# Seven block products in all six feed-forward halves of a two-block network, weight sums on GpSimd, hosted running sums in PSUM

## What is computed

```python
def sq_relu_mlp(h, w1, w2):
    return jnp.square(jax.nn.relu(h @ w1)) @ w2            # network 1, both layers: 1024 -> 4096 -> 1024

def swiglu(x, w1, w3, w2):
    return (jax.nn.silu(x @ w1) * (x @ w3)) @ w2           # network 2, layer 0: 1024 -> 2816 -> 1024

hl = layer_norm(DEEPNORM_ALPHA * hl + m_l[5] * sq_relu_mlp(modulate(hl, m_l[3], m_l[4]), ffn_w1[i], ffn_w2[i]), ...)
m_l = jnp.split((s_lat @ ada_w[i] + ada_b[i])[:, None, :], 6, axis=-1)   # six quarters of 1024 columns
m_c = jnp.split(s_ctx @ ada_w[i] + ada_b[i], 6, axis=-1)
```

## Time and profile before

| | us |
|---|---|
| median of 3 runs | 3179.68 |
| lowest, highest run | 3177.56, 3181.84 |
| profiled execution, its own time | 3183.86 |
| its span in the trace | 3182.0 |
| PE busy | 3054.5 |
| DVE busy | 1339.1 |
| ACT busy | 544.2 |
| POOL busy | 109.1 |

### The profile page before, as it was taken

The page is one execution under the profiler, slowest core; times in us unless marked ns, Lnnn a source line. Parts: engine busy times, 40 slices in busy tenths (PEclk is TensorE's granted clock), DMA queues, the critical chain, the costliest instruction groups (busy, mean ns, idle before and its releaser), DMA issues.

```text
span 3182.0 us, 33283 instructions
## 1 busy us (share of the span) xinstructions
PE 3054.5 (96%) x13304; PEld 2064.1 (65%) x13304; DVE 1339.1 (42%) x3117; ACT 544.2 (17%) x1149; POOL 109.1 (3%) x84
## 2 busy tenths in 40 slices
PE   7999989999999999899999999999999989999999
PEld 2448444444466666788844655887446666999998
DVE  3576365467647777311122327775013442000011
ACT  0115110000033434121021321000012331000000
POOL 0000000000000000000000002342000000000000
PEclk9999999999999999899999999999999988999999
DMA  7550145566331222245431104454222012887785
GB/s 260 172 172 27 53 161 183 158 186 185 116 83 50 74 80 85 101 146 152 146 93 53 53 27 161 155 171 115 73 93 80 27 53 84 275 305 267 263 293 194
DMA packets 395321, 431.58 MB, mean 136 GB/s; under 512 B 15449, under 2 KB 307960, under 8 KB 395034
## 3 DMA queue, kind: packets, MB, share of 16 engines
q1 hardware_dynamic: 294320, 329.77, 31.9%
q10 hardware_dynamic: 100842, 99.62, 9.7%
HBM read 428.32 MB, written 1.05 MB: 135 GB/s over the span
## 4 chain that ended last, share of the span: by engine, by line
PE 90%; DVE 5%; ACT 2%; issue 1%; DMA 0%; DVEq 0%; ACTq 0%
PE bank L837 45%; PE bank L2578 10%; PE bank L2159 7%; PE bank L855 5%; PE bank L2592 4%; PE bank L863 4%; PE bank L528 2%; PE bank L1951 1%; DVE arena L573 1%; PE bank L1944 1%; PE bank L2560 1%; PE bank L2604 1%; PE bank L1548 1%; PE bank L1568 1%; PE bank L1936 1%
## 5 line engine op out<-in xcount | busy, mean ns | idle before, releaser
L837 PE MATMUL bank<-uT,slot 128*128 128x512 f32 (+2 forms) x2208 | 782.8, 511 | 0.0
L837 PE MATMUL bank<-arena,slot 128*128 128x512 f32 (+1 forms) x2016 | 692.9, 505 | 12.9 <-DVEq L2758 10.6
L837 PEld LDWEIGHTS bank<-uT,slot 128*128 128x128 f32 (+1 forms) x2208 | 414.8, 190 | 319.6 <-issue 296.5
L837 PEld LDWEIGHTS bank<-arena,slot 128*128 128x128 f32 x2016 | 386.2, 193 | 298.7 <-issue 274.5
L573 DVE SCALAR_TENSOR_TENSOR arena<-arena,sT 128x256 f32<-128x256 f32 x784 | 365.4, 521 | 7.4
L2578 PE MATMUL bank<-arena,slot 128*128 128x128 f32 x2816 | 317.8, 276 | 3.3 <-issue 2.9
L2578 PEld LDWEIGHTS bank<-arena,slot 128*128 128x128 f32 x2816 | 316.8, 193 | 5.9 <-issue 5.9
L2663 DVE TENSOR_TENSOR arena<-bank,halves 128x256 f32<-128x256 f32 (+1 forms) x48 | 19.3, 403 | 433.8 <-ACT halves L2624 433.8
L916 DVE SCALAR_TENSOR_TENSOR hT<-bank,mod,hT 128x256 f32<-128x256 f32 (+1 forms) x88 | 36.8, 456 | 370.3 <-PE bank L837 370.3
L855 PE MATMUL bank<-uT,slot 128*128 128x512 f32 (+1 forms) x448 | 165.2, 530 | 5.2 <-DVE uT L600 5.2
L2592 PE MATMUL bank<-slot,arena 128*128 128x256 f32 x704 | 153.3, 379 | 1.0 <-DVEq L145 1.0
(11 more groups left out here) (362 smaller groups left out, 2770.0 us busy)
## 6 DMA issues: line engine op xcount, KB each, us to landing
arena<-in_ada_w ACTq DMA_DIRECT2D x88, 1024.0 KB, 5.3
slot<-in_ffn_w SPq DMA_DIRECT2D x42, 2048.0 KB, 8.9
slot<-in_moe_w SPq DMA_DIRECT2D x32, 2048.0 KB, 10.0
slot<-in_moe_w SPq DMA_DIRECT2D x32, 1408.0 KB, 8.6
slot<-in_moe_w SPq DMA_DIRECT2D x16, 1536.0 KB, 9.0
slot<-in_ssd_w_in SPq DMA_DIRECT2D x32, 512.0 KB, 6.7
slot<-in_gla_w_in SPq DMA_DIRECT2D x6, 2048.0 KB, 10.3
slot<-in_ev_w_in SPq DMA_DIRECT2D x6, 2048.0 KB, 7.8
```

The lines of the kernel that those rows point to most:

```text
L837: ins = pe.matmul(bank[0:m, 0:t1 - t0], w[:, k, c0:c0 + m], x[:, k, t0:t1], start=(k == 0), stop=(k == kt - 1))
```

## The change

All six halves now run on one class `Seven` with a new order of products. A unit is a weight block of 2 MB (four tiles of 128 features in the hidden halves; 16 blocks of k and 256 features in the down halves of network 1), cut in 2 x 2 quarters; tokens are cut in two halves of 256 or 128 columns. POOL writes all four weight sums over the quarters of the slot; DVE makes four token sums per stage (twice per down half, which works its k in two chunks); ACT copies the first product to its place, and DVE adds the others there. ACT does relu and square on whole units. `Down` takes the place of `Residual` in the three down halves: it is `joined`, adds chunk by chunk to `hT` from `halves`, and has its own places for the norm. Hosted pieces are spread anew over all six halves (16, 16, 6, 6, 24 and 4), their places are counted in products, their sums run in the PSUM bank `ada_rows_bank` and are made four (seven) products ahead in two (four) parts. Some constants (1408 of 2368 columns) are loaded only at the start of `OddProject`.

```diff
-            ORDER = ("11", "12", "S2", "S1", "S3", "S4", "22")
+            ORDER = ("11", "12", "S1", "22", "S2", "S4", "S3")
+            TOKENS = {"S1": 1, "22": 2, "S3": 1}
+            def order(units):
+                first = [(q, name) for q in (0, 1) for name in ("11", "12")]
+                return first + [(q, name) for q in range(units) for name in Seven.ORDER if (q, name) not in first]
+            def token_sum(self, dve, step):
+                made = S("token_sums")
+                if step > 1:
+                    dve.wait_ge(made.sem, made.made)
+                out, a, b = {1: (self.t1, self.x12, self.x11), 2: (self.t2, self.x22, self.t1),
+                             4: (self.t4, self.t2, self.x21), 3: (self.t3, self.t2, self.x11)}[step]
+                dve.tensor_tensor(out, a, b, ALU.subtract).then_inc(*made.given())
+            def product(self, pe, bank, w, name, fresh, streamed=None):
+                if name in ("S1", "S2", "S4", "S3"):
+                    pe.wait_ge(*S("weight_sums").taken("pe"))
+                if fresh and name in self.TOKENS:
+                    pe.wait_ge(*S("token_sums").taken("pe", self.TOKENS[name]))
...
+                for u in us:
+                    for k in range(self.h):
+                        if streamed and u == 0:
+                            streamed()
+                        ins = pe.matmul(bank[:, u * n:u * n + n], a[:, k, u * P:u * P + P], x[:, k, :], start=(k == 0),
+                                        stop=(k == self.h - 1))
+            def pool(pool, B, w, at):
+                pool.tensor_tensor(a21, a21, a22, ALU.add).then_inc(*made.given())
+                B.full(pool, at("11"))
+                pool.wait_ge(made.sem, made.made)
+                pool.tensor_tensor(a11, a21, a11, ALU.subtract).then_inc(*made.given())
+                B.full(pool, at("12"))
+                pool.wait_ge(made.sem, made.made)
+                pool.tensor_tensor(a12, a12, a11, ALU.subtract).then_inc(*made.given())
+                B.full(pool, at("22"))
+                pool.tensor_tensor(a22, a22, a11, ALU.subtract).then_inc(*made.given())
+            def dve(dve, B, c, at, name):
...
+                elif name == "S2":
+                    ins = dve.tensor_tensor(c.second, c.second, c.both(bank), ALU.add)
+                elif name == "S4":
+                    ins = dve.tensor_tensor(c.c12, c.c22, c.part(bank), ALU.add)
+                else:
+                    ins = dve.tensor_tensor(c.second, c.second, c.both(bank), ALU.add)
...
+        class Down(Stage):
+            joined = True
+            pooled = True
...
+            def dve(self, dve, B, ch):
+                dve.wait_ge(*self.src.made(self.chunks[0][1]))
+                self.sevens[0].token_sum(dve, 1)
+                B.full(dve, -1)
+                for step in (2, 4, 3):
+                    self.sevens[0].token_sum(dve, step)
+                if self.src.guest:
+                    self.src.guest.dve(dve, ch)
+                self.norm.dve_begin(dve, ch)
+                self.norm.dve_ctx_sums(dve, ch)
+                for i, (c, u, name) in enumerate(self.order):
+                    Seven.dve(dve, B, Tiles(self.out), self.at(c, u), name)
+                    if c and u and name == "12":
+                        self.norm.dve_tile(dve, B, ch, 2 * u - 2)
+                        self.norm.dve_tile(dve, B, ch, 2 * u - 1)
...
+                    if name in ("S4", "S3"):
+                        B.freed(dve, i)
+                        j = int(name == "S3")
+                        ins = self.add(dve, j, 2 * u + j, 0, slice(0, LAT))
+                        if self.T == TOK:
+                            ins = self.add(dve, j, 2 * u + j, 1, slice(LAT, TOK))
...
+                    part_sum = guest_bank if self.in_bank else acc
...
-        stages += [hid, Residual(I["ffn_w2"][0], hid.hid, 32, M[0], 5, TOK, False,
-                                 AdaGuest(1, 0, all_six, spread, all_six), Norm(8, M[1], 0, TOK, True))]
+        hid = HiddenRelu2(I["ffn_w1"][0], TOK, AdaGuest(ada01[0:4], spread(8, 52, 16), hidden_guest, 4, 2))
+        stages += [hid, Down(I["ffn_w2"][0], hid, M[0], 5, Norm(8, M[1], 0, TOK, True),
+                             AdaGuest(ada01[4:6] + ada10[0:2], spread(5, 50, 16), down_guest, 4, 2))]
```

More of the change, by code:

```diff
@@ L511, in sides @@
             def sides(self, n):
[L513 removed]
+                return range(self.items[n][3])
             def summed(self, n):
@@ L549, in begin, with loads, sums @@
                     self.load(act, n)
[L551 to L559 removed]
+            def loads(self, act, place):
+                n = self.at.get(place + 1)
+                if n is not None and n + 2 < self.total:
+                    self.load(act, n + 2)
+            def sums(self, dve, ch, place):
+                for n, part in self.sum_at.get(place, ()):
                     g = self.first + n
                     if 0 in part:
[L562 removed]
+                        dve.wait_ge(guest_landed[g % 2], 16 * (g // 2 + 1))
                         if n >= 2:
@@ L976, in act @@
                        .then_inc(S("bias_loads").sem, 16)
-                for i in range(32):
-                    bank = B.full(act, i)
-                    if i >= 2:
-                        act.wait_ge(*S("free_a").taken("act"))
-                    act.activation(rl[i % 2][:, 0:self.T], bank[:, 0:self.T], ACT.Relu).then_inc(*B.free(i))
-                    if self.guest:
-                        self.guest.loads(act, (i,))
-                for i in range(2):
-                    act.wait_ge(*S("free_a").taken("act"))
+                for i, (q, name) in enumerate(self.order):
+                    if name == "11":
+                        Seven.act(act, B, Tiles(self.tiles(q)), i)
+                    if self.guest:
+                        self.guest.loads(act, i)
+                    if name == "S3":
+                        B.freed(act, i)
+                        h = self.tiles(q)
+                        ch.wait(ch(act.activation(h, h, ACT.Relu)))
+                        act.activation(h, h, ACT.Square).then_inc(*S("hid_done").given())
@@ L994, in dve @@
                 if self.guest:
                     self.guest.dve(dve, ch)
-                for k in range(KD if self.ctx else 0):
-                    bank = B.full(dve, 32 + k)
-                    dve.tensor_copy(hT[:, k, LAT:TOK], bank[:, 0:CTX]).then_inc(*B.free(32 + k))
         HQ = 4
```

629 lines of the change are left out of this document (342 added, 287 removed).

## The result

The changed kernel takes **3091.8 us** (median of four runs, 3090.0 to 3099.9) beside 3180.8 of the kernel before on the same chip: a ratio of 0.9726, 95% interval 0.9707 to 0.9745, or 89 us less. A second profile of the same kernel, taken later, spans 3088.9 us, and where the two differ the text says so.

What follows compares the result with a forecast made beforehand. TensorE, busy 96%, was taken as the bound: 134.8 us less matmul time, minus 22 (hidden starts), 21 (down starts), 7 (mid-stage) and 5.6 (down ends) leaves 79 us off the 3179.7 median, so 3101 us; range 3066 to 3140.

Steps and rivals of the forecast that it cites:

- ends of down halves: Behind the last product VectorE adds both blocks before the final add and is late: 2.0, 1.3 and 2.3 us.
- Rival 4: On 128 columns weight loads set the pace: 0.118 us per record, 11 us, 3112 us; inside the range, no own chance.
- one input in PSUM is not held: VectorE instructions with one input in PSUM, host sums and block sums, are not stopped by GpSimd; host sums at 0.41 us.
- rival 3: GpSimd holds sums in PSUM too, so POOL and VectorE alternate: 182 us of price, 103 slower, 3283 us; chance 0.05.
- the term of VectorE's block sums: Per unit on 256 columns, four block sums of 512 and two of 1024 elements take VectorE 5.4 us.
- the 4 us for the first host sum: Start of down 0: first host sum, wanted at product 5 (21 us), is done near 25, a wait of 4 us.
- Rival 2: In the down halves VectorE queues, TensorE waits at hosts and banks with half clock: 35 us more, 3136 us; chance 0.19.
- the 3 us for its middle: Mid-stage of down 1: the second chunk's token sums fall beside POOL's sums, costing 3 us.
- little of the clock: Start of down 1: waits of 2.5, 1.5 and 4.5 us make 9, with little half clock.
- Rival 1: TensorE hardly waits, the sums fitting into the slack: 20 to 30 us come back, not 56; 3070 us; chance 0.14.
- The 2.5 us for a normalisation held by GpSimd's second sum: Starts of hidden halves: POOL's first S2 sum can hold the normalisation once, 2.5 us in each.
- the thin start alone: Start of hidden 1: TensorE waits 2.0 us, an estimate of about a third of hidden 0's 5.4.

Runs made afterwards that it cites:

- experiment 3: Changed kernel without GpSimd's weight sums, products taking the raw quarters: 3602.5 us, not comparable because the router caused second expert passes.
- experiment 2: Changed kernel with the hosted pieces' running sums in SBUF again instead of a PSUM bank: 3200.9 us, ratio 1.0074 against the kernel before.
- experiment 11: Changed kernel without GpSimd's weight sums in down 1 alone, its products using raw blocks: 3077.1 us, ratio 0.9675 against the kernel before.
- experiments 9: Changed kernel with each GpSimd weight sum in down 1 cut into four of 256 elements: 3083.8 us, ratio 0.9696 against the kernel before.
- experiment 4: Changed kernel without GpSimd's weight sums and without the token sums: 3063.9 us, ratio 0.9634 against the kernel before.
- experiment 5: Changed kernel with GpSimd's second sum of unit 0 started later in the hidden halves: 3091.4 us beside 3093.5 for the changed kernel.
- the halves in down 1 alone: Changed kernel with each GpSimd weight sum in down 1 cut into two of 512 elements: 3088.7 us, ratio 0.9706 against the kernel before.

## Why the prediction was right, and where two errors met

The forecast was 3101 us, 9 more than measured. Its mechanism, TensorE's records at an eighth less, waits at the starts, none in the middle of the 256-column halves, host sums free of GpSimd, came out; its distribution over the halves did not. Against the time of each half without waits (first profile; in the second, down 1 is 18.1 and the sum 44 to 45):

| what comes back, us | forecast | measured |
|---|---|---|
| hidden 0, hidden 1, gated hidden (starts) | 10 + 5.5 + 6.5 = 22 | 8.1 + 2.1 + 6.5 = 16.7 |
| down 0 (start 8, middle 4) | 12 | 2.8 |
| down 1 (start 9, middle 3) | 12 | 20.7 |
| gated half's down (start) | 4 | 4.7 |
| ends of down halves | 5.6 | 2.2 |
| sum | 55.6 | 47.1 |

- *TensorE's prices.* Right to 1%: 0.216 per record of 256 columns, 0.1125 of 128 (forecast 0.2159 and 0.1117), 0.44 and 0.88 for the host steps. Rival 4 (0.118) is out.
- *GpSimd's sums.* 2.6 us taken, 2.36 measured, above its lower end of 2.2; a sum of 512 elements takes 1.27.
- *Host sums in a bank.* 0.41 us taken; from start to start they take 0.39 in a row and 0.43 on average in hidden 0 and down 0, the same in down 0 of experiment 3 without GpSimd's sums. The term was right. (The 484 ns of the earlier trace rows and the 485 above are lengths that overlap, no price.) That "one input in PSUM is not held" was the reading on which rival 3 hung; experiment 2 shows it by its opposite. The 109 us that it costs are the host sums' holds alone; the rival's 182 us count the block sums as held too, which no run tested.
- *Down 0.* The step that failed is the term of VectorE's block sums, 5.4 us a unit in the down halves too. A unit there has half the columns of output, so the six sums are 4 x 0.42 + 2 x 0.69 = 3.0 us. VectorE is busy 157.6 of 207 us, and in the second half 84.5 of 103.5, some 21 of 26 us a unit and not 24 to 26, holds included. The slack was enough for the hosts: at the start the wait of 2.18 for the token sums came as priced (0 to 2.6), but the 4 us for the first host sum and the half clock did not, and in the middle TensorE waits 0.17. The start and the middle lose 2.8 us, not 12. Rival 2 rested on the same term.
- *Down 1.* The step that failed is the 3 us for its middle, and with it "little of the clock" for its start: TensorE waits 7.4 us up to the first host step (9 taken) and 5.6 behind it, and most of the other 7.7 us of the 20.7 is the half clock. The prediction lists what the bank does not free, token sums, final adds and the norm's sums, but counts some 2 us of GpSimd for a unit in down 0 and none here. On 128 columns the instructions are short (424 ns) and GpSimd's as long as ever (2355), so a held one takes six times its time; by experiment 11 the holds put 26 us on VectorE (77 to 103) and 16 to 19 on the half. Held back, it comes late to hosts and banks, and the granted clock over the half is 0.95 and 0.93 in the two profiles where it is 1.00 in experiments 9 and 11.
- *The other rivals.* Rival 1 (3070) had the right price of down 0 and the wrong one of down 1; with all sums left out the kernel is at 3064 (experiment 4). Rival 2 came true in down 1 alone.
- *Starts of hidden halves.* 16.7 of 22. The 2.5 us for a normalisation held by GpSimd's second sum are there nearly to the tenth in hidden 0 and the gated half (2.37, 2.45); in hidden 1 there is none (waits of 0.18 us) and no half clock, and it loses 2.1 us, what was taken for the thin start alone (2.0). In experiment 5, without the hold, hidden 0 still loses 5.9 us where 7.4 had been taken and the gated half 2.9 where 4.1 had.
- *Ends.* VectorE was hardly late from the block before: TensorE waits 0.54 us for the norm's sums behind down 1 and 0.73 behind the gated half's down.
- *Rest.* The constants' late load made VectorE wait 3.61 us at 2304.11, and TensorE not. No wait of TensorE in the six halves names a transfer.

So the sum stood by luck in one part: the errors in down 0 (9 too much) and down 1 (9 too little) cancel. It was 9 us above the time by the starts and ends.

## What to carry to other kernels

Price the holds between two engines by the length of the other engine's instruction, not by its busy share: the shorter your own instructions are, the more a hold costs, and cutting the other engine's work into smaller pieces can pay though its total grows, as the quarters did here and the halves in down 1 alone did not visibly. Keep a running sum that can't be cut where it is out of the other's way, in a PSUM bank, and judge each half of a change by itself: five halves brought 104 us, and the sixth lost 11 to 14.

## What the runs showed of the hardware that was not expected

A multiply with a single tensor input, 347 ns from SBUF to SBUF and 480 to a PSUM bank, lasted up to 2443 ns beside GpSimd in the first form and no longer than 488 in the second. GpSimd is held in turn: its sums of 1024 elements take 2.36 us alone and up to 4.10 beside VectorE, those of 256 elements 0.73 and up to 1.72. And TensorE's clock after equal waits is not equal: behind 2.18 us idle 48 records took 10.60 us, behind 2.19 us at the same place in another kernel 12.29.
